# A two-block transformer on one core: attention, mixers and the entry to block 2 are issued in another order

## The chip, the cores and the metric

The kernel runs on one core of a Trainium2 chip. The metric is the device time of one execution in microseconds (us). Its engines each run their own list of instructions in the order written: TensorE (PE) multiplies, VectorE (DVE), ScalarE (ACT) and GpSimd (POOL, here also "Pool") work on vectors, SyncE (SP) issues the loads of weights. They wait for one another only through semaphores, so an instruction that waits holds up everything behind it on its engine.

## The reference

Two blocks follow one another on 256 tokens of width 1024, all in fp32. Block 1 has two layers, each with a feed-forward, a mixer (gated MLP in the first, attention in the second) and another feed-forward, with a second stream of 256 context tokens. Block 2 has two layers of feed-forward, mixer, feed-forward. Each sublayer is modulated by a vector m = silu(c) @ w_mod + b_mod.

```python
# block 1, layer 2: attention
qkv = h_lat @ w_qkv                      # 8 query heads, 2 key heads
q_l = apply_rope(rms_norm(split_heads(qkv[..., :Q_DIM], N_HEADS), q_norm_g), cos, sin)
y_lat = merge_heads(block_attend(q_l, k_all, v_all)) @ w_o

# block 2, each layer: the mixer between its two feed-forwards
h = _modulate(_rmsnorm(x, mix_norm[l]), sh2, sc2)
proj = h @ mix_w_in[l]
a_q, a_k, a_v, b_u, c_q, c_k, c_v, c_r, c_g = jnp.split(proj, splits, axis=-1)
o_a = _merge_heads(_moba_attention(rope(rmsnorm(a_q)), rope(rmsnorm(a_k)), a_v))   # 8 heads of 64
o_b = _conformer_conv(b_u, conv_w[l], ...)    # 31 taps, 256 channels, group norm, swish
o_c = _merge_heads(_rmsnorm(_gla(c_q, c_k, c_v, log_decay), gla_out_norm[l])) * jax.nn.silu(c_r)
x = x + gt2 * (jnp.concatenate([o_a, o_b, o_c], axis=-1) @ mix_w_out[l])
```

## The kernel before

**Products.** A fp32 operand a is split into a rounded high half and the rest, and each product is three passes: high by high, high by low, low by high. A "unit" is 1 MB of weights, loaded by SyncE in two transfers of 512 KB into one of two buffers `wraw`. ScalarE makes its high half `wh` (L838), VectorE its low half `wl` (L1228), and TensorE then runs the unit's products. SyncE may load unit u only when the low half of unit u-2 is made, since that is the last reader of the buffer. `split_next` issues a low half in VectorE's list; `unit(i)` there is a low half and, after it, the work on the unit's result.

**Modulation.** The vector m of the next sublayer is computed on VectorE while the present one runs: `modulation(i)` multiplies and adds (L1201, `acc`) one quarter `mraw` (1 MB) that SyncE loads in its queue between two units. TensorE's `columns` (L2099) sum the result over the partitions and turn it into columns.

**The order of the work** is written out by hand in one function for each engine and sublayer, with tables at the head of the file (`MIX_MODS`, `ATT_MODS`: after which unit a quarter comes; `MIX_TAPS`, `MIX_POOL_TAPS`: how many of the convolution's taps are done by when). No scheduler moves anything.

**Attention** (about 1680 to 1810 us). Units 0 to 3 give queries. For a pair of heads VectorE sums the squares (L1757), Pool raises the sum to the power -1/2, VectorE scales and rotates the queries in six operations (L1763 to L1773: "a turn"; `q_0` to `q_3`), TensorE transposes them (L2525) and ScalarE copies the result out of bank 6 of the result memory. Then for each head h: TensorE's scores, VectorE's maximum (`negm`, L1788), ScalarE's exponential, VectorE's division (L1793, L1796, "normalise"), TensorE's transposes of the weights (L2551) and ScalarE's copy `ptc_h`, TensorE's product with the values (L2566). The low halves of units 6 and 7 are made here by Pool (L796) and not by VectorE.

**Mixers of block 2** (about 2230 to 2410 and 2815 to 2991 us). After `proj` come the same steps for three kinds of heads: "a" and "b" (attention, `p_a`, `p_b`), "c" (the gated linear attention, `gla`), and "conv", whose 31 taps are shared by Pool (L809 multiplies, L815 adds, into `lnp`), VectorE and TensorE. Pool also makes the powers, placed between its taps after as many as `MIX_POOL_TAPS` says. Each part's result goes to the output product as a transposed, split left operand `xh`, `xl`; its low half is made on VectorE by L1935 (`low("gla")`, `low("conv")`, `low("att")`). `out(i)` is one of the four units of the output product (L2662), taken in the order `MIX_OUT`.

**Entry to block 2** (about 2009 to 2035 us). VectorE has the last result of block 1 copied out (`y_evac`), normalises it, and TensorE transposes it (L2140) and begins block 2's first feed-forward (L2365). `keep_going` is a run of throwaway products (L2128) that read constants and are read by nobody.

## Time and profile before

| | us |
|---|---|
| median of 3 runs (lowest, highest) | 3186.99 (3184.89, 3188.21) |
| profiled execution, its own time | 3188.7 |
| its span in the trace | 3187.0 |
| TensorE busy | 3090.6 (97% of the span) |
| mean granted clock of TensorE over the span, share of full | 0.984 |
| attention, mixer 1, mixer 2, entry: length of the stretch | 104, 120, 120, 28 |

The profiled execution took 1.7 us more than the median. In the trace, a "wait" is idle time of an engine ahead of an instruction, put down to the semaphore that came last by the profile; the engine named there may have been done for long, if the true one was a transfer. The granted clock is a share of full speed, at one of two levels (1.2 and 2.4 GHz) at any moment.

### The profile page before, as it was taken

How to read it: one execution, taken by the hardware profiler on the slowest of the kernel's cores; microseconds unless marked ns; L12 is line 12 of the kernel's file. 1: busy time of each engine (PE TensorE's matmuls, PEld its weight loads, DVE VectorE, ACT ScalarE, POOL GpSimd, SP SyncE). 2: the span in 40 equal slices, each digit the busy share in tenths (PEclk: the TensorE clock that was granted, in tenths of full speed). 3: DMA queues.
4: the chain of work that ended last, by engine and by line, in shares of the span. 5: the costliest groups of instructions: out<-in, count | busy, mean ns of one | idle time of the engine just before them, and what ended most of it. 6: DMA issues, size and time to landing. Idle time of an engine off the chain costs nothing.

```text
span 3187.0 us, 46876 instructions
## 1 busy us (share of the span) xinstructions
PE 3090.6 (97%) x19420; PEld 2751.5 (86%) x19420; DVE 2041.7 (64%) x2146; ACT 957.7 (30%) x1006; POOL 669.5 (21%) x616
## 2 busy tenths in 40 slices
PE   8999999999999999999997999999989999998999
PEld 5888889888888888888886798899879999997899
DVE  5844368666387434774556766675887758668664
ACT  2211122212222122221224433333533333354333
POOL 1311100224022010220102021330632313136110
PEclk9999999999999999999998999999999999999999
DMA  7633235332255332553523496685547868654464
GB/s 258 211 133 93 92 119 187 105 102 75 91 158 176 101 96 89 160 183 119 172 96 119 128 272 221 194 266 195 185 149 219 258 200 271 232 191 167 137 182 158
DMA packets 501669, 522.81 MB, mean 164 GB/s; under 512 B 15732, under 2 KB 433830, under 8 KB 501478
## 3 DMA queue, kind: packets, MB, share of 16 engines
q1 hardware_dynamic: 498536, 513.76, 50.4%
q0 software_dynamic: 2944, 6.32, 1.0%
q8 instruction: 144, 2.36, 0.3%
q14 instruction: 45, 0.37, 0.0%
HBM read 518.97 MB, written 1.05 MB: 163 GB/s over the span
## 4 chain that ended last, share of the span: by engine, by line
PE 86%; DVE 7%; POOL 3%; ACT 2%; DMA 1%; issue 1%; SPq 0%; DVEq 0%; ACTq 0%; POOLq 0%
PE ps L2191 29%; PE ps L2365 15%; PE ps L2277 15%; PE ps L2389 8%; PE ps L2219 6%; PE ps L2256 2%; DVE wl L1228 2%; PE ps L2235 1%; POOL wst L809 1%; PE ps L2662 1%; PE ps L2128 1%; POOL lnp L815 1%; PE ps L2303 1%; PE ps L2099 1%; DMA mraw<-in_ada_w 1%
## 5 line engine op out<-in xcount | busy, mean ns | idle before, releaser
L1228 DVE TENSOR_TENSOR wl<-wraw,wh 128x2048 fp32r<-128x2048 f32 x339 | 829.0, 2446 | 566.9 <-ACT wh L838 561.7
L838 ACT ACTIVATE wh<-wraw 128x2048 fp32r<-128x2048 f32 x341 | 652.5, 1913 | 945.7 <-PE ps L2277 387.5
L2191 PE MATMUL ps<-xh,wh 128*128 128x512 f32 (+1 forms) x1504 | 564.9, 376 | 0.5 <-DVE xl L1280 0.3
L2191 PE MATMUL ps<-xl,wh 128*128 128x512 f32 (+1 forms) x1504 | 552.7, 367 | 0.0
L2191 PE MATMUL ps<-xh,wl 128*128 128x512 f32 (+1 forms) x1504 | 551.3, 367 | 0.0
L2365 PE MATMUL ps<-xh,wh 128*128 128x258 f32 x1408 | 403.7, 287 | 5.3 <-DVE xl L1426 4.2
L2365 PE MATMUL ps<-xh,wl 128*128 128x258 f32 x1408 | 399.7, 284 | 0.0
L2365 PE MATMUL ps<-xl,wh 128*128 128x258 f32 x1408 | 399.3, 284 | 0.0
L673 POOL CAST hh<-ht 128x256 f32 (+1 forms) x176 | 140.1, 796 | 1227.1 <-DVE ht L1608 891.0
L1201 DVE SCALAR_TENSOR_TENSOR acc<-mraw,svec,acc 128x1024 f32<-128x1024 f32 x259 | 342.3, 1341 | 12.7 <-DMA mraw<-in_ada_w 5.2
L2191 PEld LDWEIGHTS ps<-xl,wh 128*128 128x128 f32 x1504 | 283.2, 188 | 49.3
L2191 PEld LDWEIGHTS ps<-xh,wl 128*128 128x128 f32 x1504 | 283.4, 188 | 44.9 <-issue 0.7
L2191 PEld LDWEIGHTS ps<-xh,wh 128*128 128x128 f32 x1504 | 283.6, 189 | 44.7 <-issue 1.4
L2365 PEld LDWEIGHTS ps<-xh,wh 128*128 128x128 f32 x1408 | 268.6, 191 | 10.3 <-DVE xl L1426 7.1
L2365 PEld LDWEIGHTS ps<-xl,wh 128*128 128x128 f32 x1408 | 269.0, 191 | 0.0
L2365 PEld LDWEIGHTS ps<-xh,wl 128*128 128x128 f32 x1408 | 268.7, 191 | 0.0
L2219 PE MATMUL ps<-wh,xh 128*128 128x256 f32 x832 | 241.4, 290 | 13.1 <-DVE wl L1228 13.1
L936 ACT ACTIVATE sg<-ps 128x512 f32<-128x512 f32 (+1 forms) x88 | 47.9, 545 | 662.3 <-PE ps L2191 629.8
L2219 PE MATMUL ps<-wl,xh 128*128 128x256 f32 x832 | 235.2, 283 | 0.0
L2219 PE MATMUL ps<-wh,xl 128*128 128x256 f32 x832 | 235.1, 283 | 0.0
L674 POOL TENSOR_TENSOR hl<-ht,hh 128x256 f32 (+1 forms) x176 | 214.5, 1219 | 29.1 <-POOL hh L673 29.1
L2277 PE MATMUL ps<-wh,hh 128*128 128x512 f32 x520 | 205.3, 395 | 1.3 <-DVE wl L1228 1.3
(430 smaller groups left out, 5564.6 us busy)
## 6 DMA issues: line engine op xcount, KB each, us to landing
wraw<-in_ffn_w_in SPq DMA_DIRECT2D x352, 512.0 KB, 5.2
wraw<-in_ffn_w_out SPq DMA_DIRECT2D x176, 512.0 KB, 4.2
mraw<-in_ada_w SPq DMA_DIRECT2D x72, 1024.0 KB, 7.0
mraw<-in_w_mod SPq DMA_DIRECT2D x64, 1024.0 KB, 6.8
wraw<-in_gmlp_w_in SPq DMA_DIRECT2D x48, 512.0 KB, 4.5
wraw<-in_mix_w_in SPq DMA_DIRECT2D x48, 512.0 KB, 4.7
wraw<-in_gmlp_w_out SPq DMA_DIRECT2D x24, 512.0 KB, 3.9
first_w<-in_w_mod SPq DMA_DIRECT2D x8, 1024.0 KB, 11.6
```

Of the source, the lines that this page charges most:

```text
L673: steps.link(pool.tensor_copy(hh[:, where], ht[:, par, 0:width]))
L674: pool.tensor_tensor(hl[:, where], ht[:, par, 0:width], hh[:, where].bitcast(F32), ALU.subtract)\
L838: act.activation(wh[:, slot], wraw[:, slot], ACT.Copy).then_inc(whi_done, 1)
L936: act.activation(sg[:, pair, 0:W], ps[:, 2 * pair, 0:W], ACT.Silu).then_inc(sg_ready, 1)
L1201: op = dve.scalar_tensor_tensor(out=to, in0=mraw[:, q % 2, jj], scalar=svec[:, v, 2 * q + jj:2 * q + jj + 1], in1=biasrow[:] if q == jj == ...
L1228: dve.tensor_tensor(wl[:, slot], wraw[:, slot], wh[:, slot].bitcast(F32), ALU.subtract)\
L2191: m = pe.matmul(ps[:, bank, 0:width], a, b, start=k == p == 0, stop=k == KD - 1 and p == 2)
L2219: m = pe.matmul(to, a, b, start=k == p == 0, stop=k == KD - 1 and p == 2)
L2256: m = pe.matmul(ps[:, 2 * t + half], a, b, start=False, stop=i == kk == 1 and p == 2, skip_group_check=i == 0)
L2277: m = pe.matmul(ps[:, bank0 + 2 * t + half], a, b, start=start and kk == p == 0, stop=stop and kk == 1 and p == 2, skip_group_check=not st ...
L2365: m = pe.matmul(ps[:, 2 * pair + r, 0:XW], a, b, start=n == p == 0, stop=n == KD - 1 and p == 2)
L2389: m = pe.matmul(ps[:, j, 0:T], a, b, start=i == kk == p == 0, stop=i == KF // 2 - 1 and kk == 1 and p == 2, skip_group_check=i == 5)
```

## The change

- **Attention.** The sums of squares are issued one unit ahead of the turns. The turn of `q_2` comes ahead of the first maximum, that of `q_3` after the third head's maximum in the loop over heads. Pool's two low halves go to VectorE, after heads 2 and 4. The second query unit is transposed through bank 7. ScalarE makes the high halves of units 5 and 6 earlier in its list, and an exponential of one column is put in ahead of unit 5.
- **Mixers.** Low halves move ahead of sums and statistics, and the quarters of modulation come after them. Pool's powers come after 7 and 10 taps instead of 9 and 13. ScalarE instead of VectorE copies the linear attention's output, squares it, and copies the turned weights; small activations of one column stand ahead of changes of its function. TensorE's output products wait for the copied convolution and no longer for its statistics. The columns of modulation move behind the scores and behind the last output product.
- **Entry to block 2.** 20 throwaway products run before the wait for `y_evac` and 36 after it, then the transposes, then the columns; before, the wait came first, then the columns, 16 throwaways, and the transposes.

The order in three places, before and after. First VectorE's list in attention, from the first head's maximum on (negm, from the scores in ps); nrm holds sums of squares, ql queries, den and sg or ht the softmax. Before:

```order
L1788 TENSOR_REDUCE negm<-ps 128x2
L1757 TENSOR_REDUCE nrm<-tm 128x4
L1483 TENSOR_SCALAR nrm<-nrm 128x4
L1763 TENSOR_TENSOR ql<-ql,nrm 128x2x256
L1768 TENSOR_TENSOR tm<-ql,wst 128x256
L1769 TENSOR_TENSOR tm<-ql,wst 128x256
L1770 TENSOR_TENSOR ql<-ql,wst 128x2x2x64
L1771 TENSOR_TENSOR ql<-ql,wst 128x2x2x64
L1772 TENSOR_TENSOR ql<-ql,tm 128x2x2x64
L1773 TENSOR_TENSOR ql<-ql,tm 128x2x2x64
L1793 RECIPROCAL den<-den 128x2
L1796 TENSOR_SCALAR sg<-sg,den 128x512 x2
```

After:

```order
L1786 TENSOR_TENSOR ql<-ql,tm 128x2x2x64
L1805 TENSOR_REDUCE negm<-ps 128x2
L1770 TENSOR_REDUCE nrm<-tm 128x4
L1496 TENSOR_SCALAR nrm<-nrm 128x4
L1810 RECIPROCAL den<-den 128x2
L1813 TENSOR_SCALAR sg<-sg,den 128x512 x2
L1805 TENSOR_REDUCE negm<-ps 128x2
L1810 RECIPROCAL den<-den 128x2
L1813 TENSOR_SCALAR ht<-ht,den 128x512 x2
L1805 TENSOR_REDUCE negm<-ps 128x2
L1776 TENSOR_TENSOR ql<-ql,nrm 128x2x256
```

The seven operations on ql no longer stand between the first maximum and the first division; the sum of `q_3` (nrm) alone does. The turn of `q_2` ends in the first row; that of `q_3` begins in the last.

Second, VectorE's list in each mixer, behind the turn of the queries (proj); modc and acc belong to modulation, nrm to the next heads' sum. Before:

```order
L1916 TENSOR_TENSOR proj<-proj,om 128x2x8x32
L1917 TENSOR_TENSOR proj<-proj,om 128x2x8x32
L1221 COPY modc<-ps 128x8
L1201 SCALAR_TENSOR_TENSOR acc<-mraw,svec,biasrow 128x1024
L1201 SCALAR_TENSOR_TENSOR acc<-mraw,svec,acc 128x1024
L1899 TENSOR_REDUCE nrm<-om 128x16
L1483 TENSOR_SCALAR nrm<-nrm 128x16
L1228 TENSOR_TENSOR wl<-wraw,wh 128x2048
L1201 SCALAR_TENSOR_TENSOR acc<-mraw,svec,acc 128x1024 x2
L1889 SCALAR_TENSOR_TENSOR wst<-lnp,wst 128x256 x3
L1907 TENSOR_TENSOR proj<-proj,nrm 128x2x512
```

After:

```order
L1937 TENSOR_TENSOR proj<-proj,om 128x2x8x32
L1938 TENSOR_TENSOR proj<-proj,om 128x2x8x32
L1239 TENSOR_TENSOR wl<-wraw,wh 128x2048
L1920 TENSOR_REDUCE nrm<-om 128x16
L1496 TENSOR_SCALAR nrm<-nrm 128x16
L1232 COPY modc<-ps 128x8
L1212 SCALAR_TENSOR_TENSOR acc<-mraw,svec,biasrow 128x1024
L1212 SCALAR_TENSOR_TENSOR acc<-mraw,svec,acc 128x1024
```

The low half wl of unit 7 has moved ahead of the sum and of two operations of modulation; the three taps (L1889) are no longer here.

Third, VectorE's list at the end of each mixer; lnp is the convolution, BN_STATS and BN_AGGR its statistics, xl the low half of the linear attention's result. Before:

```order
L1930 TENSOR_TENSOR sg<-sg,den 128x1024
L1921 TENSOR_REDUCE negm<-ps 128x4
L2048 COPY lnp<-ps 128x512
L2051 BN_STATS x<-lnp 128x6 x8
L2054 BN_AGGR x<-x 128x2 x8
L2056 TENSOR_SCALAR x<-x 128x8
L2059 TENSOR_TENSOR lnp<-lnp,x 128x512
L1935 TENSOR_TENSOR xl<-ps,xh 128x2x256
```

After:

```order
L1951 TENSOR_TENSOR sg<-sg,den 128x1024
L1239 TENSOR_TENSOR wl<-wraw,wh 128x2048
L2067 COPY lnp<-ps 128x512
L2070 TENSOR_TENSOR om<-om,gg 128x2x256
L1942 TENSOR_REDUCE negm<-ps 128x4
L1956 TENSOR_TENSOR xl<-ps,xh 128x2x256
L2074 BN_STATS x<-lnp 128x6 x8
L2077 BN_AGGR x<-x 128x2 x8
L2079 TENSOR_SCALAR x<-x 128x8
```

L1935 (now L1956) has moved ahead of sixteen BN operations and two that follow them. A low half of weights (L1239) has come in ahead of the convolution's copy.

```diff
@@ -55,7 +55,7 @@
 MIX_TAPS = (0, 0, 0, 6, 12, 18, 24, 31, 31, 31, 31, 31)
-MIX_POOL_TAPS, MIX_DVE_TAPS = (9, 13, 24), (24, 28, 31)
+MIX_POOL_TAPS, MIX_DVE_TAPS = (7, 10, 24), (24, 28, 31)
@@ -308,6 +308,7 @@
 nrm_g = place[:, 1944:1952]
+table_scrap = place[:, 1768:1772]
 tm_ang = place[:, 1880:1944].rearrange("p (t f) -> p t f", t=TT)
@@ -790,11 +791,6 @@
             power(nrm1[:, 4 * u:4 * u + 4], 4)
-        for i in (6, 7):
-            u = s["n_unit"] + i
-            pool.wait_ge(whi_done, u + 1)
-            pool.tensor_tensor(wl[:, u % 2], wraw[:, u % 2], wh[:, u % 2].bitcast(F32), ALU.subtract)\
-                .then_inc(wlo_done, 1)
     elif s["kind"] == "mix":
@@ -1001,7 +997,8 @@
             AP_.wait(act, "q_%d" % u, 0)
-            AA.done("qt_%d" % u, act.activation(qt1[:, 2 * u:2 * u + 2].rearrange("p a b -> p (a b)"), ps[:, 6], ACT.Copy))
+            AA.done("qt_%d" % u, act.activation(qt1[:, 2 * u:2 * u + 2].rearrange("p a b -> p (a b)"),
+                                                ps[:, 7 if u == 1 else 6], ACT.Copy))
@@ -1024,15 +1021,17 @@
         unit(3, False)
+        square(1)
         split_next(u0 + 4)
-        square(1)
-        copy_heads(0)
         unit(4, False)
         square(2)
+        copy_heads(0)
+        split_next(u0 + 5)
+        act.activation(nrm1[:, 31:32], ones[:, 0:1], ACT.Exp)
+        unit(5, False)
+        square(3)
         copy_heads(1)
         exps(0)
-        unit(5)
-        square(3)
         copy_heads(2)
@@ -1075,8 +1074,8 @@
                     act.activation(proj[:, :, at:at + CW], src, ACT.Copy).then_inc(pair_free, 1)
-            if i == 2:
-                split_next(u0 + 3)
+            if i in (2, 5, 6):
+                split_next(u0 + i + 1)
             if i < 10:
@@ -1136,8 +1135,8 @@
         square(1)
-        unit(6)
-        unit(7)
+        unit(6, False)
+        unit(7, False)
         split_next(u0 + 8)
@@ -1148,13 +1147,25 @@
         unit(10)
+        MP.wait(act, "o", turn)
+        stage("o_copy", act.activation(om[:, :, 768:1024], ps[:, 6].rearrange("p (t c) -> p t c", t=TT), ACT.Copy))
+        stage("o_sq", act.activation(hx[:], om[:, :, 768:1024], ACT.Square))
         exps("c", 2, p_c, 0)
-        unit(11)
+        split_next(u0 + 11)
         exps("b", 4, p_b, 8)
+        act.activation(table_scrap[:, 0:1], ones[:, 0:1], ACT.Silu)
+        unit(11, False)
+        act.activation(table_scrap[:, 1:2], ones[:, 0:1], ACT.Exp)
         MP.wait(act, "omt", turn)
...
         exps("a", 0, p_a[:], 12)
+        act.activation(table_scrap[:, 2:3], ones[:, 0:1], ACT.Silu)
+        MP.wait(act, "pt_c", turn)
+        MA.done("pt_c", act.activation(pt0[:, :, :, 0:P], ps[:, 2:4].rearrange("p r (h q) -> p r h q", h=4), ACT.Copy))
         unit(12)
+        MP.wait(act, "pt_b", turn)
+        act.activation(pt0[:, :, 2:4, P:2 * P], ps[:, 2].rearrange("p (r h q) -> p r h q", r=2, h=2), ACT.Copy)
+        MA.done("pt_b", act.activation(pt1[:, :, 2:4], ps[:, 3].rearrange("p (r h q) -> p r h q", r=2, h=2), ACT.Copy))
         MV.wait(act, "o_conv", turn)
@@ -1449,6 +1460,8 @@
                 take_chunk(s, n + 2)
+            if n == 5 and s["kind"] == "mix":
+                mod_end(nxt, 2, 3)
             low_chunk(nxt, n)
@@ -1776,11 +1789,15 @@
-        def queries(u):
-            part = nrm1[:, 4 * u:4 * u + 4]
-            sums("%d" % u, tm1[:, 2 + u % 2].rearrange("p (n d) -> p n d", d=HD), part)
-            dve.wait_ge(rstd_ready, n_power[0])
-            turn(ql[:, :, u * CW:(u + 1) * CW], part, 0, "q_%d" % u)
+        asked = {}
+        def query_sums(u):
+            sums("%d" % u, tm1[:, 2 + u % 2].rearrange("p (n d) -> p n d", d=HD), nrm1[:, 4 * u:4 * u + 4])
+            asked[u] = n_power[0]
+        def query_turn(u):
+            dve.wait_ge(rstd_ready, asked[u])
+            turn(ql[:, :, u * CW:(u + 1) * CW], nrm1[:, 4 * u:4 * u + 4], 0, "q_%d" % u)
@@ -1814,19 +1831,28 @@
         turn(ql[:, :, 1024:1280], k_part[:, 0:4], 1, "k_turned")
+        query_sums(0)
         unit(3)
-        queries(0)
+        query_turn(0)
+        query_sums(1)
         unit(4)
-        queries(1)
+        query_sums(2)
+        query_turn(1)
+        query_turn(2)
         maximum(0)
-        queries(2)
+        query_sums(3)
         normalise(0)
         maximum(1)
-        queries(3)
         normalise(1)
...
                 maximum(h + 2)
+            if h == 0:
+                query_turn(3)
+            elif h == 2:
+                unit(5)
+            elif h == 4:
+                unit(6)
             if h in ATT_MODS:
@@ -1834,7 +1860,6 @@
                 normalise(h + 2)
-        dve.wait_ge(wlo_done, u0 + 9)
         unit(7)
@@ -1857,12 +1882,8 @@
                 mod_end(nxt, 0, 6, 480)
-            if i == 9:
-                mod_end(nxt, 1, 6, 488)
             if i == 12:
                 factors(nxt)
-            if i == 15:
-                mod_end(nxt, 2, 3)
             for sec, q in mix_mods(i):
@@ -1974,20 +1995,19 @@
         turn_heads(0)
+        split_next(u0 + 6)
+        sum_squares(1)
         modulation(5)
-        sum_squares(1)
-        unit(6)
-        taps(1)
         turn_heads(1)
         split_next(u0 + 7)
-        split_next(u0 + 8)
-        modulation(7)
         MA.wait(dve, "decays", turn)
...
         stage("qk", dve.tensor_tensor(kt[:], c_k, e2[:], ALU.mult))
-        modulation(8)
+        modulation(6)
+        split_next(u0 + 8)
+        modulation(7)
         for j in range(2):
@@ -2004,7 +2024,9 @@
         stage("kt_t", op)
-        unit(9)
+        modulation(8)
+        split_next(u0 + 9)
+        mod_end(nxt, 1, 6, 488)
         MP.wait(dve, "scores", turn)
@@ -2024,29 +2046,30 @@
         stage("states", op)
-        unit(10)
+        split_next(u0 + 10)
+        taps(1)
+        modulation(9)
         maximum("c", 2, 8, 0)
-        MP.wait(dve, "o", turn)
+        MA.wait(dve, "o_sq", turn)
         o_c = om[:, :, 768:1024]
-        stage("o_copy", dve.tensor_copy(o_c, ps[:, 6].rearrange("p (t c) -> p t c", t=TT)))
-        steps.link(dve.tensor_tensor(hx[:], o_c, o_c, ALU.mult))
         groups = nrm_g.rearrange("p (t h) -> p t h", t=TT)
...
         maximum("b", 4, 4, 8)
-        unit(11)
         dve.wait_ge(rstd_ready, n_power[0])
...
                                      ALU.mult))
+        normalise("c", p_c, 0)
+        split_next(u0 + 11)
+        MP.wait(dve, "conv", turn)
+        stage("conv_c", dve.tensor_copy(ctok.rearrange("p a b -> p (a b)"), ps[:, 7]))
+        grp = ctok.rearrange("p t (g c) -> p (t g) c", c=64)
         MA.wait(dve, "silu", turn)
         stage("oc", dve.tensor_tensor(o_c, o_c, gg[:], ALU.mult))
-        normalise("c", p_c, 0)
         maximum("a", 0, 4, 12)
-        MP.wait(dve, "conv", turn)
-        steps.link(dve.tensor_copy(ctok.rearrange("p a b -> p (a b)"), ps[:, 7]))
-        grp = ctok.rearrange("p t (g c) -> p (t g) c", c=64)
+        low("gla", 6, (6,))
         for g in range(8):
@@ -2057,10 +2080,8 @@
         stage("stats", dve.tensor_tensor(grp, grp, hmv[:, :, 0:1].broadcast_to([P, 8, 64]), ALU.subtract))
-        low("gla", 6, (6,))
-        MP.wait(dve, "pt_c", turn)
-        MV.done("pt_c", dve.tensor_copy(pt0[:, :, :, 0:P], ps[:, 2:4].rearrange("p r (h q) -> p r h q", h=4)))
         normalise("b", p_b, 8)
+        normalise("a", p_a[:], 12)
         dve.wait_ge(rstd_ready, n_power[0])
@@ -2068,16 +2089,15 @@
         stage("o_conv", last)
-        normalise("a", p_a[:], 12)
-        turned_weights("b", 2, slice(2, 4))
         turned_weights("a", 0, slice(0, 2))
...
         low("conv", 4, (2,))
+        split_next(u0 + 13)
+        low("att", 0, (0, 1))
+        modulation(10)
+        split_next(u0 + 14)
         modulation(12)
-        unit(13)
-        low("att", 0, (0, 1))
-        unit(14)
-        unit(15)
+        modulation(13)
     if s["block"] == 1 and not two(nxt):
@@ -2336,10 +2356,11 @@
     elif s["i"] == B2:
+        keep_going(3, 20)
         pe.wait_ge(y_evac, s["n_group"])
+        keep_going(3, 36)
+        transposes(s)
         columns(s, 2)
-        keep_going(3, 16)
-        transposes(s)
     now[:] = halves_of(s)
@@ -2516,13 +2537,13 @@
             AV.wait(pe, "q_%d" % u, 0)
-            if u in (1, 2):
-                AA.wait(pe, "qt_%d" % (u - 1), 0)
+            if u == 2:
+                AA.wait(pe, "qt_0", 0)
             elif u == 3:
...
                 for t in range(TT):
-                    m = pe.transpose(ps[:, 6, h * T + t * P:h * T + (t + 1) * P],
+                    m = pe.transpose(ps[:, 7 if u == 1 else 6, h * T + t * P:h * T + (t + 1) * P],
                                      ql[:, t, (2 * u + h) * HD:(2 * u + h + 1) * HD], ident[:])
@@ -2554,7 +2575,9 @@
             AA.wait(pe, "ptc_%d" % h, 0)
-            if h == 1:
+            if h == 0:
+                AA.wait(pe, "qt_1", 0)
+            elif h == 1:
                 AA.wait(pe, "qt_2", 0)
@@ -2665,8 +2688,6 @@
             m.then_inc(w_used, 1)
-            if i == 2:
-                columns(nxt, 2, 3)
@@ -2744,8 +2765,6 @@
         unit(9)
-        pe.wait_ge(mcol_done, sections(nxt, 0) + 1)
-        columns(nxt, 1, 6, 488)
         taps(9)
@@ -2761,6 +2780,8 @@
         MP.done("scores", m)
+        pe.wait_ge(mcol_done, sections(nxt, 0) + 1)
+        columns(nxt, 1, 6, 488)
         unit(10)
@@ -2792,14 +2813,14 @@
         MA.wait(pe, "exp_b", turn)
-        MV.wait(pe, "stats", turn)
+        MV.wait(pe, "conv_c", turn)
         out(0)
-        MV.wait(pe, "pt_c", turn)
+        MA.wait(pe, "pt_c", turn)
         MV.wait(pe, "norm_b", turn)
...
         MP.done("pt_a", turn_weights(p_a[:], 0))
-        MV.wait(pe, "pt_b", turn)
+        MA.wait(pe, "pt_b", turn)
         MA.wait(pe, "conv", turn)
@@ -2816,6 +2837,7 @@
             out(i)
+        columns(nxt, 2, 3)
 for n in range(8):
```

## Rows read from the trace of the kernel before

**Rows 1.** The page's part 1: busy time and share of each engine.
```profile
PE 3090.6 (97%) x19420; PEld 2751.5 (86%) x19420; DVE 2041.7 (64%) x2146; ACT 957.7 (30%) x1006; POOL 669.5 (21%) x616
```
**Rows 2.** TensorE's waits: line, releaser, us in total, times, longest.
```profile
PE ps L2662 <- DVE xl L1935: 19.8, 4, 6.1
...
PE ps L2219 <- DVE wl L1228: 13.1, 8, 4.3
...
PE ps L2551 <- DVE ht L1796: 7.3, 1, 7.3
PE ps L2525 <- DVE ql L1773: 6.0, 1, 6.0
```
**Rows 3.** Stretches: length, busy (x instructions) of five engines, TensorE clock, DMA share, GB/s.
```profile
1706.00:1810.00 104.00, 82.79 (x414) 63.04 (x413) 74.47 (x108) 40.50 (x66) 14.25 (x8) 0.90 0.32 108
2294.00:2414.00 120.00, 100.61 (x722) 92.53 (x721) 93.31 (x123) 42.62 (x77) 47.55 (x34) 0.90 0.42 139
2876.00:2996.00 120.00, 102.07 (x759) 94.32 (x757) 98.49 (x129) 44.95 (x79) 48.52 (x35) 0.93 0.42 141
2008.00:2036.00 28.00, 23.21 (x134) 21.60 (x133) 20.20 (x34) 8.53 (x15) 4.58 (x6) 0.76 0.27 84
```
**Rows 4.** VectorE on tile ql: ns min/median/max of the five turns' first two operations.
```profile
L1763 DVE TENSOR_TENSOR ql<-ql,nrm x5: 691/694/4992, 1701.7 to 1735.7; 128x512 f32<-128x512 f32 x5
L1768 DVE TENSOR_TENSOR tm<-ql,wst x5: 424/426/4597, 1702.4 to 1740.7; 128x256 f32<-128x256 f32 x5
```
**Rows 5.** GpSimd's timeline in attention: start us, us, line, operation.
```profile
1735.61 9.41 POOL L796 TENSOR_TENSOR wl<-wraw,wh 128x2048 fp32r<-128x2048 f32 x2
```
**Rows 6.** TensorE's timeline in attention; in brackets the idle time before.
```profile
1737.94 1.44 PE L2566 MATMUL ps<-ptb,ql 128*128 128x256 f32 x4 [2.92 <-ACT ptb L1043]
...
1748.39 1.97 PE L2551 MATMUL ps<-ident,ht 128*128 128x128 f32 x8 [7.30 <-DVE ht L1796]
```
**Rows 7.** ScalarE's timeline in attention.
```profile
1735.07 1.91 ACT L838 ACTIVATE wh<-wraw 128x2048 fp32r<-128x2048 f32 x1
```
**Rows 8.** DMA issues around attention: count, KB each, median us to landing.
```profile
mraw<-in_w_mod SPq DMA_DIRECT2D x4, 1024.0 KB, 6.3
```
**Rows 9.** TensorE's timeline in the second mixer.
```profile
2883.65 0.58 PE L2219 MATMUL ps<-wh,xh 128*128 128x256 f32 x1 [4.33 <-DVE wl L1228]
...
2931.91 0.60 PE L2785 MATMUL ps<-ident,lnp 128*128 128x128 f32 x4
...
2947.18 0.55 PE L2662 MATMUL ps<-xh,wh 128*128 128x256 f32 x1 [4.33 <-DVE xl L1935]
...
2971.70 0.55 PE L2662 MATMUL ps<-xh,wh 128*128 128x256 f32 x1 [5.00 <-DVE xl L1935]
```
**Rows 10.** VectorE's timeline in the second mixer.
```profile
2870.96 1.22 DVE L1907 TENSOR_TENSOR proj<-proj,nrm 128x1024 f32<-128x1024 f32 x1 [5.47 <-POOL nrm L670]
...
2946.34 0.69 DVE L1935 TENSOR_TENSOR xl<-ps,xh 128x512 fp32r<-128x512 f32 x1
```
**Rows 11.** GpSimd's timeline in the second mixer: the end of its taps.
```profile
2920.64 0.74 POOL L820 TENSOR_TENSOR lnp<-lnp,wst 128x256 f32<-128x256 f32 x1
```
**Rows 12.** GpSimd's taps of both mixers: ns min/median/max, first and last start.
```profile
L809 POOL TENSOR_SCALAR wst<-lnp x46: 921/1762/3895, 2262.8 to 2918.8; 128x256 f32<-128x256 f32 x46
L815 POOL TENSOR_TENSOR lnp<-lnp,wst x46: 722/1142/2670, 2263.8 to 2919.8; 128x256 f32<-128x256 f32 x46
```
**Rows 13.** TensorE's timeline at the entry to block 2.
```profile
2011.44 3.37 PE L2099 MATMUL ps<-ones,acc 128*128 128x1 f32 x16 [2.38 <-DVEq L1323]
2014.67 5.65 PE L2128 MATMUL ps<-ident,ones 128*128 128x128 f32 x32
...
2024.17 0.36 PE L2365 MATMUL ps<-xh,wh 128*128 128x258 f32 x1 [2.11 <-DVE xl L1426]
```
**Rows 14.** VectorE at that entry: the last normalising step.
```profile
2016.56 1.53 DVE L1360 TENSOR_SCALAR x<-x,mv,rstd 128x1024 f32<-128x1024 f32 x2 [0.84 <-POOL rstd L670]
```
**Rows 15.** TensorE at the entry to attention: 16 throwaway products at full clock.
```profile
1672.91 3.73 PE L2128 MATMUL ps<-ident,ones 128*128 128x128 f32 x32
```

14 lines of the change are left out of this document (7 added, 7 removed).

## The prediction

> **What bounds the kernel now.** I read the page's busy table first. TensorE is busy for 97% of the span, VectorE for 64%, the others for less [rows 1]. So a change in order can give back only two things: TensorE's idle time, and work that ran at a low clock behind it. Next I read TensorE's waits over the whole span. Four lines of them lie in the stretches that the diff touches: 19.8 us in four waits of the mixers' output products for a low half `xl`, 13.1 us in eight waits for low halves of weights, 7.3 us for head 1's weights, 6.0 us for `q_2` [rows 2]. Third, the table of stretches gives the whole of it: in attention TensorE is busy 82.79 of 104 us, in the mixers 100.61 and 102.07 of 120, at the entry 23.21 of 28, with a mean granted clock of 0.90, 0.90, 0.93 and 0.76 [rows 3]. Idle time is thus 21.2, 19.4, 17.9 and 4.8 us, 63 us in all. The level is either full or half, so a mean of 0.90 over 104 us is about 21 us at half clock; some of those are idle anyway, the others lose half of themselves. Last I read the timelines of the engines that end each wait [rows 4 to 14].
>
> **Attention, -9 us.** VectorE's turn of `q_3` contains two operations of 4.99 and 4.60 us whose medians are 0.69 and 0.42 [rows 4]. In the same time Pool's weight subtraction takes 9.41 us, started 0.06 us before them [rows 5]. The excess, 4.3 + 4.2 = 8.5 us, stands right ahead of head 1's division in VectorE's list, and TensorE waits 7.30 us for that [rows 6]. The change takes away both ends of this: the subtraction is VectorE's now, and the turn of `q_3` is behind three maxima. So 7.3 goes. The wait for `q_2`, 6.0 [rows 2], goes too: its turn now stands ahead of the first maximum, and its power is asked for a unit earlier.
> Low clock: of some 21 us at half level I count 13 as idle; the other 8 or 9 lose half, 4.5 us. Sum of what can be had: 17.8.
> Against it: head 0's maximum comes behind a turn of one operation of 0.69 and six of 0.42, 3.2 us [rows 4]; between 0 and that I take 1.3. Two low halves in VectorE's loop over heads, formerly Pool's: they cost what its idle time there doesn't cover, taken as 0.8. SyncE's queue: the load of unit 9 needs unit 7's low half, which now comes after head 4, and a quarter of modulation is loaded behind it. A quarter of 1 MB takes 6.3 us to land with nothing before it [rows 8]; VectorE will ask for the third one early, hold up the maximum behind it, and so TensorE. I take 4.3 us (0 to 6.3). Another dip of the clock from these waits: 2.4. ScalarE still makes a high half of 1.91 us ahead of head 0's copy [rows 7], so the wait of 2.92 [rows 6] stays. 17.8 - 1.3 - 0.8 - 4.3 - 2.4 = 9.0. Ends: all the costs absent, 16; every cost at its upper end and no clock back, 3.
>
> The Trainium skill says in *SBUF — State Buffer* (section "SBUF: two separate sides") that VectorE and GpSimd share a port pair as an exclusive lock, the loser being blocked for the whole instruction. By that rule the trace agrees: two short operations end with the long one of Pool.
>
> **The mixers, -18.4 and -15.9 us.** The second one shows the chain. VectorE's sum for the second turn asks Pool for a power, and Pool has taps ahead of it: VectorE stands idle 5.47 us until 2870.96 [rows 10]. It then turns, does two pieces of modulation, and makes unit 7's low half, for which TensorE waits 4.33 us at 2883.65 [rows 9]. The change asks Pool after 7 taps instead of 9. A tap is a multiplication and an addition, median 1.76 + 1.14 = 2.9 us [rows 12], so the power comes 5.8 us earlier, of which the sum's own place lets about 4.5 through; and the low half stands ahead of the sum and of a modulation's copy and products. Together it comes about 9 us sooner, and the wait of 4.33 goes. At the end of the mixer `out(0)` waits 4.33 and `out(2)` 5.00 us for `xl` [rows 9]. The first of these low halves runs at 2946.34 for 0.69 us [rows 10], behind the statistics, and needs nothing of them; the second stood behind modulation. Both have moved ahead. What is left of the idle time lies in smaller waits behind the same two chains.
> So I take the idle time as the whole that can be had, 19.4 and 17.9, and of the clock: a mean of 0.90 over 120 us is 12 us lost at most, 0.93 is 8.4, part of that on idle time; I take 7 and 6. Then I leave 8 us in each: 0.7 for the first `xl` itself [rows 10], about 1 for the copies that ScalarE now makes in a list with others, 0.5 at the feed-forward behind, up to 1.5 for Pool (below), 1 for a dip of the clock, and 3 because VectorE has little room: it is busy 98.49 us of the 120 [rows 3], and some 4 us of copies and squares leave it, so a stretch of 102 us would see it busy for 94 and any late input of it shows. 19.4 + 7 - 8 = 18.4; 17.9 + 6 - 8 = 15.9.
> The moved modulation quarters cost VectorE nothing more in sum; they lie beside TensorE's output products, and part of them behind the mixer, where it has room (64% busy over the span, [rows 1]). ScalarE gets one copy, one square, two copies of weights and small activations with their table loads, all from VectorE's side, with 30% busy [rows 1]. Pool's taps end at 2920.64 + 0.74 = 2921.4 [rows 11]; TensorE's transposes of them begin at 2931.91 [rows 9]. With 4.33 and about 4 of other idle time gone ahead of them, TensorE arrives at about 2923.6, so Pool is early by 2 us or, with denser neighbours, late by 1.5.
> Ends of the unknown: each mixer 10 (half of it turned into other waits) to 25 (nothing left over but the rest of the low clock).
>
> **The entry, +0.5 us.** Before: a wait of 2.38, columns of 3.37, 16 throwaways of 5.65 at 2014.67, the transposes, a wait of 2.11 for `xl`, and the first unit at 2024.17 [rows 13]. At full clock 16 of them take 3.73, 0.23 each [rows 15]. Now 20 (4.7 us) begin 2.38 before 2011.44, and cover that wait with 2.3 to spare; 36 more are 8.4, so the transposes begin at about 2022, against 2020.3, though VectorE's last normalising step ends at 2018.1 [rows 14]. That costs 1.7. The columns now lie in the wait of 2.11 and cost some 0.5 beyond it. Back come the part of the first unit at a full clock, 1.5 to 2, since TensorE has not stood still before it (the mean is 0.76 now, [rows 3]). Net +0.5, between -2.5 (more of the unit at full clock) and +2.
>
> In *TensorE: Matmul & The Clock Gate*, section "Part 4: PE-mode transpose", the Trainium skill says that transposes don't count as activity for the clock. Then the 16 transposes behind the throwaways would bring the clock down again ahead of the first unit, and the entry would cost 1.5 to 2 us; no row here separates that.
>
> **Sum.** -9.0 - 18.4 - 15.9 + 0.5 = -42.8, against the profiled execution's 3188.7: 3145.9. That execution lies 1.7 above the median of 3187.0, so 3144 beside the median.
>
> **Rivals.**
> A, half of it in the mixers. When the low halves come early, VectorE's and Pool's lists are denser and slow each other. Pool's longest tap operations are 3.90 and 2.67 us, its shortest 0.92 and 0.72 [rows 12], which shows how wide this is. For it: the 98.49 busy us of VectorE [rows 3] would be nearly the whole of a shorter stretch. Against it: each of the four large waits has one named instruction that no longer stands in front. Gain 9 + 10 + 10 = 29: 3158. Chance 0.29.
> B, the clock holds throughout and the quarter in attention is not late: -16, -23, -23 and +1: 3126. For it: TensorE would have no wait above 2 us left. Against it: some new wait has mostly taken an old one's place. Chance 0.14.
> C, slower: Pool's taps become the bound. TensorE needs all of Pool's taps before the transposes at 2931.91 [rows 9]. Pool's powers come earlier and push 14 to 17 taps behind them, beside a VectorE that now works there without a pause. If Pool ends at 2931.9, 10.5 after its present end, the gain ahead of the transposes is gone; 17 taps do that at 10.5 / 17 = 0.6 more each, 3.5 us instead of 2.9. The kernel becomes slower than before when the mixers lose 4.3 us each in place of gaining about 17, so at some 21 us behind TensorE's new arrival: 23 after Pool's present end, 1.4 more a tap, 4.3. At 4.6 a tap it is -9 + 0.5 + 2 x 8 = +7.5: 3194.5. The two longest together are 6.6 [rows 12], so it could be. Against it: the medians sum to 2.9, and the shared-side stalls were long only where a whole weight tile was subtracted [rows 4, 5], as none is on Pool now. Chance 0.06.
> D, it does not do what it says: each moved low half still waits for a load or high half behind it in another queue, and the waits reappear at the same size. Only attention's 7.3 would go: 3180. Chance 0.02.
>
> **Numbers.** The forecast has 0.49, A 0.29, B 0.14, C 0.06, D 0.02. What can be told from no change is about 0.2%, 6.4 us: faster is under 3180.6, slower over 3193.4. The forecast, A, B and half of D are faster; of C a third is within the 0.2%. Faster 0.93, same 0.03, slower 0.04. Range: the lower ends of the gains are 3 + 10 + 10 - 2 = 21 (3164), the upper 16 + 25 + 25 + 2 = 68 (3117); not all of them fall together, and I leave 1 in 10 on either side: 3123 to 3165.
>
> **What would show it.** In the profile after: VectorE's operations of a turn all near 0.69 and 0.42, none over 2; no wait of TensorE at the product that transposes `q_2`; the clock in attention over 0.95. In the mixers: unit 7's product behind less than 1 us of wait, the sum of waits for `xl` at the output product under 7 instead of 19.8, busy time of over 112 in what were 120 us, a clock of 0.97. The wait for Pool's taps ahead of the transposes at most 2 us. In attention a wait for a quarter `mraw` in VectorE's third modulation, which was not there. At the entry no idle time before the throwaways and a first unit without its half-speed part. I am wrong if VectorE waits for scores or powers at the same places a few us later, if Pool's tap chain ends last at the transposes, or if the stretches keep a mean clock of 0.90 though their waits have gone.

## The result and the profile after

The changed kernel takes 3137.16 us (median of 4 runs, 3135.3 to 3143.24), the kernel before 3185.94 on the same chips (4 runs). The ratio is 0.985, with a 95% interval of 0.9833 to 0.9867: 49 us less, between 42 and 53. The profiled execution took 3135.57, against 3188.7 before.

The page after, busy time and share of each engine, the row of [rows 1]:

```profile
PE 3076.2 (98%) x19500; PEld 2740.4 (87%) x19500; DVE 2031.9 (65%) x2138; ACT 965.0 (31%) x1023; POOL 668.9 (21%) x614
```

TensorE's waits after (line, releaser: us in total, times, longest), which answer to [rows 2]; L2685 is the output product, L2239 the product of attention and mixers, L2572 the transposes of attention's weights, L2589 the product with the values:

```profile
PE ps L2572 <- DVE ht L1813: 4.9, 1, 4.9
PE ps L2589 <- ACT ptb L1042: 4.9, 4, 2.5
PE ps L2239 <- DVE wl L1239: 3.7, 5, 1.0
...
PE ps L2685 <- DVE xl L1956: 1.5, 2, 0.8
```

The 19.8 us ahead of the output products are 1.5, the 13.1 ahead of L2239 are 3.7, and the wait for the third query pair is in no row. One wait of 4.9 us is new in kind, though it stands at the same line as the 7.3 of before.

To see where the time came from, each stage is cut at the same product in both kernels; attention runs from the transposes at L2580 (L2603 after) to the seventh product at L2277 (L2297 after). Length, busy time of the five engines, granted clock, DMA share, GB/s; attention, mixer 1, mixer 2 in the kernel before:

```profile
1706.27:1779.80 73.53, 54.24 (x281) 40.39 (x279) 56.22 (x85) 34.48 (x62) 13.40 (x6) 0.86 0.30 108
2242.92:2416.64 173.72, 153.25 (x1115) 142.07 (x1113) 137.11 (x180) 77.25 (x129) 80.25 (x55) 0.93 0.51 175
2869.16:2998.12 128.96, 111.03 (x826) 103.05 (x825) 104.20 (x135) 49.60 (x82) 55.88 (x39) 0.93 0.42 142
```

The same in the changed kernel, and the entry over 28 us as in [rows 3]:

```profile
1703.30:1769.57 66.27, 53.67 (x280) 40.42 (x279) 52.39 (x85) 34.69 (x63) 3.59 (x4) 0.93 0.33 121
2230.88:2380.15 149.27, 143.37 (x1115) 134.20 (x1114) 134.20 (x175) 80.78 (x137) 81.38 (x55) 0.99 0.61 203
2832.69:2944.93 112.24, 107.22 (x827) 100.58 (x826) 97.93 (x128) 53.06 (x95) 56.91 (x40) 0.95 0.51 167
2002.00:2030.00 28.00, 27.52 (x209) 26.61 (x208) 18.90 (x34) 9.16 (x16) 7.56 (x10) 0.88 0.28 84
```

Read a row as length less TensorE's busy time (idle), and busy time against busy time with as many matmuls (what the clock gives back). Attention is 7.3 us shorter, 6.7 of it idle time and 0.6 clock. Mixer 1 is 24.4 shorter: its idle time falls from 20.5 to 5.9, and the same 1115 records take 153.25 and then 143.37 us. Mixer 2 is 16.7 shorter, 12.9 of idle time and 3.8 of clock.

The stages sum to 47.5 us less (the entry is 0.9 longer), while the two profiled spans differ by 53.1. The other 6 us lie where TensorE's products are the same in both: 2.9 ahead of attention, where only the kernel before was at half clock around 45 and 448 us, and 3.2 between the entry and mixer 1, where it was at half clock around 2230 us. They belong to these two executions and not to the change.

The same cuts through every run, with the us of the stage at the half clock in brackets; "entry" is a stretch of 79 us from the feed-forward ahead of the entry (1954.4 in the kernel before) into block 2's first feed-forward (2033.4):

| run | median us | attention | entry | mixer 1 | mixer 2 |
|---|---|---|---|---|---|
| before | 3186 | 73.5 (20.5) | 79.0 (13.7) | 173.7 (23.9) | 129.0 (17.1) |
| after | 3137.2 | 66.3 (9.7) | 79.9 (6.8) | 149.3 (3.4) | 112.2 (10.2) |
| e1_att_only | 3174.5 | 66.4 (9.6) | 77.5 (10.2) | 173.6 (23.9) | 129.0 (17.1) |
| e2_mix_only | 3143.3 | 76.4 (17.1) | 79.4 (13.7) | 150.0 (6.8) | 110.9 (6.8) |
| e3_entry_only | 3184.5 | 74.0 (20.5) | 78.6 (0) | 168.2 (17.1) | 129.1 (17.1) |
| e4_powers_only | 3178.6 | 76.2 (17.1) | 77.5 (10.2) | 164.5 (13.7) | 122.6 (10.2) |
| e5_quarter | 3132.0 | 58.9 (0) | 80.2 (6.8) | 150.0 (6.8) | 108.7 (3.4) |
| e6_entry22 | 3134.4 | 66.5 (9.9) | 75.5 (3.4) | 151.8 (10.2) | 109.6 (6.8) |
| e7_powers_back | 3152.4 | 66.1 (5.8) | 80.4 (6.8) | 158.0 (10.2) | 117.2 (6.8) |
| e8_halves_only | 3182.3 | 72.5 (16.3) | 78.1 (10.2) | 172.7 (23.9) | 128.9 (17.1) |
| e9_gla_behind | 3151.4 | 67.0 (10.2) | 78.7 (0) | 162.2 (20.5) | 116.8 (13.7) |
| e10_att_behind | 3140.4 | 66.4 (9.7) | 79.7 (3.4) | 156.0 (13.7) | 109.9 (6.8) |
| e11_entry0 | 3140.7 | 66.8 (10.2) | 78.5 (17.1) | 149.2 (3.4) | 112.4 (10.2) |
| e12_best | 3129.0 | 58.9 (0) | 76.8 (6.8) | 151.9 (10.2) | 110.3 (6.8) |

Three cautions come with it. Each row is one profiled execution, and that of e4 was the shortest of its 11 (3169.0 against a median of 3178.6). The clock moves by itself: mixer 1 has the same instructions in before and in e3_entry_only, yet it is 5.5 us shorter there, with 6.8 us less at half clock. And equal brackets don't make equal stages: attention has the same instructions in before, e3, e2 and e4, and takes 73.5, 74.0, 76.4 and 76.2 us. The longer two have less time at half clock, but head 1's wait is 8.5 us in them and not 7.3. So a difference of a few us between two such rows proves nothing alone; the medians and intervals settle it, taken as ratios, since the kernel before was measured beside each group of runs and its own median lay between 3182.5 and 3186.5.

### The profile page after: what moved, and what is told of

It reads as the page before. It is cut to its first block, busy times and chain, and to the rows that moved or that the text cites. A ratio compares the mean times of both kernels' runs of the same rounds, so it can differ in the third digit from the quotient of the medians.

```text
span 3133.9 us, 47043 instructions
## 1 busy us (share of the span) xinstructions
PE 3076.2 (98%) x19500; PEld 2740.4 (87%) x19500; DVE 2031.9 (65%) x2138; ACT 965.0 (31%) x1023; POOL 668.9 (21%) x614
## 4 chain that ended last, share of the span: by engine, by line
PE 91%; DVE 5%; ACT 2%; issue 1%; DMA 1%; SPq 0%; POOL 0%; DVEq 0%; ACTq 0%
PE ps L2211 30%; PE ps L2386 16%; PE ps L2297 15%; PE ps L2239 8%; PE ps L2410 8%; PE ps L2276 2%; PE ps L2255 1%; DVE wl L1239 1%; PE ps L2148 1%; PE ps L2323 1%; PE ps L2653 1%; PE ps L2119 1%; PE ps L2685 1%; PE ps L2513 1%; ACT wh L834 1%
## 5 line engine op out<-in xcount | busy, mean ns | idle before, releaser
L1239 DVE TENSOR_TENSOR wl<-wraw,wh 128x2048 fp32r<-128x2048 f32 x341 | 833.7, 2445 | 567.9 <-ACT wh L834 562.7
L2239 PE MATMUL ps<-wh,xh 128*128 128x256 f32 x832 | 239.4, 288 | 3.7 <-DVE wl L1239 3.7
L2239 PE MATMUL ps<-wl,xh 128*128 128x256 f32 x832 | 233.4, 281 | 0.0
L2239 PE MATMUL ps<-wh,xl 128*128 128x256 f32 x832 | 233.4, 281 | 0.0
L2297 PE MATMUL ps<-wh,hh 128*128 128x512 f32 x520 | 205.2, 395 | 1.3 <-DVE wl L1239 1.3
```

Source lines behind the costliest of these rows:

```text
L1239: dve.tensor_tensor(wl[:, slot], wraw[:, slot], wh[:, slot].bitcast(F32), ALU.subtract)\
L2239: m = pe.matmul(to, a, b, start=k == p == 0, stop=k == KD - 1 and p == 2)
L2297: m = pe.matmul(ps[:, bank0 + 2 * t + half], a, b, start=start and kk == p == 0, stop=stop and kk == 1 and p == 2, skip_group_check=not st ...
```

## The experiments

**The three parts, one at a time.** Each is the kernel before with the hunks of one part of the diff.

e1_att_only:

> The kernel before with the attention part of the change alone. Theory (the parts act apart from one another, and the two traces' landmarks give each its share): attention 7.1 us shorter by the landmarks, so a time 7 below the kernel before, the wait of 7.3 us for head 1's weights and that of 6.0 for the third query pair gone, a wait of some 5 us for a late quarter of modulation in their place. Rival 1 (the forecast's own size): 9 below. Rival 2 (the freed time is taken back by the clock): within 2 us of before.

3174.48 us (4 runs), ratio 0.9962 (0.9946 to 0.9977): 12 us less, between 7.3 and 17. By the cut attention is 7.2 shorter, and TensorE's two waits are replaced by one of 4.8 for the late quarter, as the theory had it. The forecast's 9 lies in the interval and the theory's 7.1 just under its lower end; rival 2 is out, the clock takes nothing back.

e2_mix_only:

> The kernel before with the mixers' part alone. Theory: the landmarks give 27 us in the first mixer (3 of them a dip of the clock at its start that the change has nothing to do with) and 17 in the second, so 41 to 44 below the kernel before. Rival 1 (the forecast's sizes): 34 below. Rival 2 (a share of it belongs to the entry's or attention's part, by the clock or the queue of loads): under 30 below.

3143.32 us (4 runs), ratio 0.9863 (0.9848 to 0.9878): 44 us less, between 39 and 48. The mixers' part alone is nearly the whole, and the two cuts, 23.7 and 18.1 us shorter, are those of the changed kernel within the clock's own movement. The theory's 41 to 44 holds; the forecast's 34 is too small.

e3_entry_only:

```diff
+keep_going(3, 20)
 pe.wait_ge(y_evac, s["n_group"])
+keep_going(3, 36)
+transposes(s)
 columns(s, 2)
-keep_going(3, 16)
-transposes(s)
```

> The kernel before with the entry's part alone. Theory: 36 throwaway products behind the wait end 3.3 us after the normalised x is there, so the first unit starts later, and it still runs at half clock: 1.1 to 1.3 us slower than before. Rival 1: the forecast's 0.5 slower. Rival 2: with the units behind it at full clock it gives time back, 1 to 2 us faster.

3184.54 us (11 runs), ratio 0.9994 (0.9985 to 1.0003): no difference that can be told. The interval reaches from 5 us faster to 1 slower: the forecast's +0.5 and rival 2 (1 to 2 faster, as the median is) lie in it, the theory's 1.1 to 1.3 slower just outside. Its profiled execution shows the entry at a clock of 1.00 over 28 us, where the changed kernel, with the same instructions, has 0.88; so the theory's "still at half clock" did not hold in it either. The three parts sum to 12 + 44 + 2 = 58 us against 49 together; with intervals of some 5 us either way on each, that is no proof of a loss between them.

**Attention: which operation blocked which.**

```diff
-for i in (6, 7):                         # GpSimd
-    pool.wait_ge(whi_done, u + 1)
-    pool.tensor_tensor(wl[...], wraw[...], wh[...], ALU.subtract)
+if h == 2: unit(5)                       # VectorE, in the loop over heads
+elif h == 4: unit(6)
```

e8_halves_only:

> The kernel before with one thing changed: the two low halves of weights that Pool made in attention are made by VectorE, after heads 2 and 4; all sums and turns stay where they were. Theory (Pool's long operation blocks VectorE's short ones): the two operations of 4.99 and 4.60 us fall to 0.69 and 0.42, TensorE's wait of 7.30 goes, the wait of 6.0 for the third query pair stays, the late quarter comes in: attention 3 us shorter or less. Rival 1 (they were long for another reason, such as their place in the list): they stay long. Rival 2: the late quarter eats all of it and the clock more, no change or slower.

3182.29 us (12 runs), ratio 0.9997 (0.9988 to 1.0005): no change that can be told, 4 us less at most. The mechanism is as the theory said. VectorE's first two operations of the five turns, ns min/median/max, which answer to [rows 4]:

```profile
L1758 DVE TENSOR_TENSOR ql<-ql,nrm x5: 691/691/694, 1701.8 to 1735.7; 128x512 f32<-128x512 f32 x5
L1763 DVE TENSOR_TENSOR tm<-ql,wst x5: 424/425/426, 1702.5 to 1736.4; 128x256 f32<-128x256 f32 x5
```

The turn of `q_3` stands where it stood, and with Pool's subtractions gone both long operations are gone. [Rows 5] holds two subtractions (x2), and the trace has them apart: 4.51 us from 1735.61 and 4.93 from 1740.08. VectorE's operation of 4.99 began 0.06 us after the first, that of 4.60, at 1740.70, 0.6 after the second; each ended 0.3 to 0.5 us after its own. That TensorE gains nothing is seen in the waits of its timeline in the same stretch:

```profile
1728.53 1.11 PE L2523 MATMUL ps<-ident,ql 128*128 128x128 f32 x4 [6.00 <-DVE ql L1768]
...
1774.46 1.97 PE L2549 MATMUL ps<-ident,ht 128*128 128x128 f32 x8 [4.99 <-DVE ht L1791]
```

The wait of 7.30 is gone, the one of 6.00 stays, and 4.99 us come in near the end. The late quarter eats nearly all of it, as rival 2 has it; the cut is 1.0 us shorter. The Trainium skill's rule, *SBUF — State Buffer*, section "SBUF: two separate sides", of an exclusive lock between VectorE and GpSimd, agrees with these rows: 4.99 and 4.60 us with a subtraction at work each [rows 4], 0.69 and 0.42 without.

**The late quarter.** In the changed kernel VectorE waits in the loop, and behind it TensorE:

```profile
1761.26 2.60 DVE L1212 SCALAR_TENSOR_TENSOR acc<-mraw,svec,acc 128x1024 f32<-128x1024 f32 x2 [5.66 <-DMA mraw<-in_w_mod]
```

```profile
1765.25 1.97 PE L2572 MATMUL ps<-ident,ht 128*128 128x128 f32 x8 [4.93 <-DVE ht L1813]
```

SyncE's queue shows why: one run of loads that ends at 1754.24 with the last weight unit, which had to wait for unit 7's low half (made from 1750.86), and only then both quarters:

```profile
1743.54 10.64 SPq L515 DMA_DIRECT2D wraw<-in_attn_w_o  x4
1754.24 0.94 SPq L500 DMA_DIRECT2D mraw<-in_w_mod  x2
```

e5_quarter changes one number:

```diff
-ATT_MODS, ATT_LOADS = (1, 3, 5, 6), (5, 5, 9, 9)
+ATT_MODS, ATT_LOADS = (1, 3, 5, 6), (5, 5, 8, 9)
```

> The changed kernel with one load moved: the third quarter of modulation is loaded ahead of the attention's last weight unit instead of behind it. Theory (the wait of 5.66 us of VectorE for that quarter, and TensorE's 4.93 behind it, come from the place in SyncE's queue, behind a load that waits for unit 7's low half): VectorE's wait and TensorE's wait of 4.93 gone, attention 5 us shorter, up to 8 with the dip of the clock behind it, so 3130 to 3133. Rival (VectorE would wait at the same place for another input, or the weight unit comes late instead): TensorE waits 2 us or more at the last units, and the time stays within 2 us of the changed kernel.

3131.99 us (4 runs), ratio 0.9844 (0.983 to 0.9858). The queue now has the quarter at 1741.70, between the two weight units, VectorE's wait for it is gone, and what remains is 1.11 us for the fourth, which TensorE doesn't feel:

```profile
1740.85 0.81 SPq L515 DMA_DIRECT2D wraw<-in_attn_w_o  x2
1741.70 0.43 SPq L500 DMA_DIRECT2D mraw<-in_w_mod  x1
1750.47 0.81 SPq L515 DMA_DIRECT2D wraw<-in_attn_w_o  x2
1751.33 0.43 SPq L500 DMA_DIRECT2D mraw<-in_w_mod  x1
```

```profile
1700.84:1759.73 58.89, 49.84 (x279) 37.72 (x279) 52.57 (x86) 34.72 (x63) 4.04 (x4) 1.00 0.37 135
```

Attention is 58.9 us long instead of 66.3, 7.4 less. The wait of 4.93 is gone, and waits for low halves of the query units are 1.3 longer, so 3.6 are idle time; 3.8 are the clock, now at full all through it (9.7 us at half before). The time can't show it: the medians differ by 5 us, the ratios by 2 only, and the intervals overlap. That TensorE's wait hung on the place in the queue is shown by the trace; what it is worth in time is not.

**The mixers: the power.** e4_powers_only is the kernel before with one line changed; e7_powers_back is the changed kernel with that line as before:

```diff
-MIX_POOL_TAPS, MIX_DVE_TAPS = (9, 13, 24), (24, 28, 31)
+MIX_POOL_TAPS, MIX_DVE_TAPS = (7, 10, 24), (24, 28, 31)
```

> The kernel before with one line changed: Pool's powers come after 7 and 10 taps instead of 9 and 13. Theory: VectorE's wait of 5.47 us before the second turn shrinks, and with it each mixer's wait for unit 7's low half of 4.3 us: 4 to 9 us faster in all. Rival 1 (the low half waits for what else stands ahead of it in VectorE's list): under 2 us. Rival 2 (Pool's later taps become the bound at the transposes of its sum): slower.

> The changed kernel with Pool's powers after 9 and 13 taps again. Theory (the earlier power is one needed link of the mixers' chain): VectorE's wait ahead of the second turn comes back with 3 to 5 us, TensorE waits at unit 7 to 9 or at the heads' transposes, 2 to 4 us in each mixer, 4 to 8 slower in all. Rival 1 (with the low halves ahead of the sums, VectorE's wait for the power lies beside work of TensorE and costs nothing): within 2 us. Rival 2 (Pool's later taps held up the end): faster.

e4: 3178.64 us (11 runs), ratio 0.9979 (0.9969 to 0.9988): 7 us faster, between 4 and 10. VectorE turns two groups of heads in each mixer, and it is the first turn (the prediction and the expectations call it the second) that waited for Pool. In mixer 1 its idle time there falls from 5.48 us to 0.56, and TensorE's eight waits for low halves of weights fall from 13.1 us, the longest 4.3, to 7.1, the longest 1.2; the output products' 19.8 stay at 19.6:

```profile
2281.14 1.23 DVE L1907 TENSOR_TENSOR proj<-proj,nrm 128x1024 f32<-128x1024 f32 x1 [0.56 <-POOL nrm L670]
```

```profile
PE ps L2219 <- DVE wl L1228: 7.1, 8, 1.2
```

e7: 3152.42 us (5 runs), ratio 0.9903 (0.989 to 0.9916), against 0.985 with the line: 15 us slower than the changed kernel by the medians and 17 by the ratios, roughly 10 to 24, more than the 4 to 8 of the theory, and some twice what the line gives in the kernel before. VectorE's timeline and TensorE's waits in e7:

```profile
2277.50 1.23 DVE L1928 TENSOR_TENSOR proj<-proj,nrm 128x1024 f32<-128x1024 f32 x1 [5.49 <-POOL nrm L671]
...
2293.80 1.23 DVE L1928 TENSOR_TENSOR proj<-proj,nrm 128x1024 f32<-128x1024 f32 x1 [2.83 <-POOL nrm L671]
```

```profile
PE ps L2754 <- DVE proj L1938: 9.3, 2, 4.7
...
PE ps L2239 <- DVE wl L1239: 5.9, 7, 2.3
```

The first row is the first turn, with the stall of before; the second turn now waits too, for the second power. With the low half moved ahead of the second turn, TensorE waits less for low halves and more for the turned heads themselves (L2754), 4.7 us in each mixer. The late power is the same stall in both kernels; the other moves took away what else TensorE would have waited for.

**The mixers: the two low halves at the end.**

```diff
-low("gla", 6, (6,))                      # e9: behind the statistics again
 for g in range(8): ... bn_stats, bn_aggr ...
 stage("stats", ...)
+low("gla", 6, (6,))
```

```diff
-low("att", 0, (0, 1))                    # e10: behind two operations
 modulation(10)
+low("att", 0, (0, 1))
```

> The changed kernel with the linear attention's low half behind the convolution's statistics again, all else as changed. Theory (TensorE's wait at out(0) is set by what stands ahead of this low half in VectorE's list): the four kinds of statistics operations, 1.10 + 0.65 + 0.17 + 0.74 and gaps, 2.9 us, come ahead of it, TensorE's wait at out(0) goes from 0.77 to 3.6 in each mixer, 6 to 8 us slower in all with the clock. Rival (out(0) would wait anyway, for its high half or for the weights): the wait stays under 2 us, no change.

> The changed kernel with the attention heads' low half behind the two modulation operations that now follow it. Theory: it is made 2.6 us later (two operations of 1.3), TensorE takes it up at once at out(2), so a wait of about 2.5 us comes back in each mixer, 5 to 7 us slower in all with the clock. Rival 1 (there is slack at out(2)): under 2 us. Rival 2 (VectorE would have to wait there for the quarter's load too, as it did 3.17 us in the kernel before): over 5 us in each mixer.

e9: 3151.39 us (4 runs), ratio 0.9894 (0.987 to 0.9918): 14 us slower than the changed kernel by both measures, roughly 5 to 23. The wait is what the four operations are worth, 2.9 us more in each mixer:

```profile
PE ps L2685 <- DVE xl L1956: 7.4, 2, 3.7
```

The time is more than twice the wait, though the theory's 6 to 8 is within the noise. The cuts say where it lies: mixer 1 is 12.9 us longer, with 20.5 us at half clock against 3.4, mixer 2 is 4.5 longer. How much of that low clock the waits brought, and how much this one execution had anyway, isn't shown.

e10: 3140.37 us (4 runs), ratio 0.9861 (0.9841 to 0.9881): no difference from the changed kernel can be told, though the interval would allow the theory's 5 to 7. The trace decides: the wait that the theory adds is not there, so rival 1 holds. The low half is made 2.4 us later, counted from `out(0)`, and TensorE takes it up with no wait:

```profile
2365.75 1.22 DVE L1956 TENSOR_TENSOR xl<-ps,xh 128x1024 fp32r<-128x1024 f32 x1
```

```profile
2366.87 0.28 PE L2685 MATMUL ps<-xl,wh 128*128 128x256 f32 x1
2367.11 0.36 PE L2685 MATMUL ps<-xh,wh 128*128 128x256 f32 x1
```

It ends at 2366.97, and the unit that needs it begins at 2367.11, behind the product of 2366.87, as it would have. So `out(2)` had about 2.5 us of slack, used up to the last. What made 5.00 us of wait before [rows 9] is shown by VectorE's rows ahead of that low half in the kernel before:

```profile
2960.96 2.60 DVE L1201 SCALAR_TENSOR_TENSOR acc<-mraw,svec,acc 128x1024 f32<-128x1024 f32 x2 [0.21 <-DVE prea L1267]
...
2967.82 2.60 DVE L1201 SCALAR_TENSOR_TENSOR acc<-mraw,svec,acc 128x1024 f32<-128x1024 f32 x2 [2.05 <-DMA mraw<-in_ada_w]
```

Two pieces of modulation stood in front of it, 5.2 us, and the second waited for its own load, 2.05 us here and 3.17 in mixer 1 (where TensorE's wait was 6.10). Without the load's 2.05 some 2.95 of the 5.00 would have been left, an estimate from these rows. One piece fits into the slack of 2.5, as e10 shows; two pieces and the load did not.

**The entry.** e6_entry22 is the changed kernel with `keep_going(3, 22)` behind the wait in place of 36; e11_entry0 has neither the 20 nor the 36.

> The changed kernel with 22 throwaway products behind the wait at the entry to block 2 instead of 36. Theory (they end 3.3 us after the last normalising step): transposes 3.2 us earlier, the first unit as much earlier, at half clock as now: the entry 3 us shorter. Rival 1 (the throwaways also carry the clock): more of the first units runs at half clock, and 1 to 3 us of that are lost again. Rival 2: VectorE's first operations behind the transposes set the pace, no change.

> The changed kernel with no throwaway products at the entry to block 2 at all. Theory (the first unit runs at half clock whether they are there or not, and TensorE's place is set by x): the transposes begin when x is ready, 3.3 us earlier than with 36, and the time is that of 22 throwaways, or up to 2 us longer for more half clock. Rival (they carry the clock through): 3 to 7 us slower than with 22, with a low clock from the wait on for 10 us or more.

In the changed kernel x is ready at 2008.2 (VectorE's last step begins at 2006.69 and takes 1.53), and the transposes begin at 2011.52, right behind the throwaways:

```profile
1999.01 12.67 PE L2148 MATMUL ps<-ident,ones 128*128 128x128 f32 x112
2011.52 1.91 PE L2160 MATMUL ps<-ident,x 128*128 128x128 f32 x16
```

e6: 3134.36 us (4 runs), ratio 0.9849 (0.9835 to 0.9863); the interval holds the changed kernel's 0.985. By the cut the entry is 4.4 us shorter than in the changed kernel, 3.2 of it the 14 throwaways at 0.23 each, the rest clock (3.4 us at half against 6.8), so the theory's 3 holds and rival 1's loss is not seen. That stands in the trace and not in the times. e11: 3140.67 us (4 runs), ratio 0.9858 (0.9838 to 0.9878), no difference from the changed kernel either. TensorE stands 9.20 us before the transposes, and these and the columns take 3.65 and 3.41 us, at half clock:

```profile
2012.36 3.65 PE L2160 MATMUL ps<-ident,x 128*128 128x128 f32 x16 [9.20 <-issue]
2015.80 3.41 PE L2119 MATMUL ps<-ones,acc 128*128 128x1 f32 x16
```

17.1 us are at half clock there, against 0 to 6.8 in the six kernels with 56 throwaways and 3.4 and 6.8 in the two with 42. That is the rival's picture and not the theory's: the throwaways do carry the clock. The entry is 78.5 us long, against 78.6 to 80.4 with 56 and 75.5 and 76.8 with 42: 36 behind the wait delay as much as they save, 22 come out ahead. This rests on one trace each; the times don't tell the three apart.

**Both together.** e12_best has the lines of e5 and e6.

> The changed kernel with both the earlier load of the third quarter and 22 throwaways instead of 36. Theory (the two act apart): 7 to 9 us less in attention and 3 to 4.5 less at the entry by the stages, so about 3126, under both kernels. Rival (the granted clock takes part of it back): 3130 to 3134.

3128.98 us (5 runs, 3128.27 to 3136.16), ratio 0.9831 (0.9813 to 0.9848): 54 us below the kernel before and, by the medians, 8 below the changed kernel, by the ratios 6. The intervals overlap (the changed kernel's is 0.9833 to 0.9867), so that last gain is not shown beyond the noise. Attention is 58.9 us again, 7.4 less than in the changed kernel, and the entry 76.8, 3.1 less, both as the theory had them. It has the lowest median of all runs here; the theory's 3126 was 3 too low, and the rival's 3130 to 3134 a little too high.

## Why the prediction was right

- **Direction, size and time.** 3144 was forecast, in a range of 3123 to 3165; 3137 came. 42.8 us against 49 (42 to 53). Part of the closeness is luck: attention and the entry gave 2 us less than written down and the mixers 7 more, and mixer 1's share moves by itself. Measured against its 168.2 us in e3, where it has the instructions of before, its gain is 19.0 and not 24.4.
- **Attention, -9.** 7.3 by the cut. The wait of 7.30 was Pool's doing (e8), the one of 6.0 went, head 0's new wait was put at 1.3 and is 1.49 us at TensorE, and the late quarter, put at 4.3, is 4.93. Idle time fell by 6.7 where these terms give 6.9. What was too large is the clock: 0.6 came back where 4.5 less a dip of 2.4 was written. The forecast took Pool's 9.41 us for one subtraction; it was two, one behind each long operation, which changes nothing in the sum. The quarter could have been had: e5 shows it was one place in a queue.
- **The mixers, -18.4 and -15.9.** 24.4 and 16.7, and together 44 in e2. The chain was right link by link: VectorE's wait for Pool's power ahead of the first turn is 0.55 us in mixer 2 instead of 5.47, of the waits of 4.33 that at unit 7 is gone and that at `out(0)` 0.77, and that of 5.00 at `out(2)` is gone. The term that was mis-sized is what is left over. 8 us were written down for each mixer, 3 of them because VectorE would be too dense. Idle time left is 5.9 and 5.0 in a longer cut, and VectorE, busy for 134.20 of 149.27 us and 97.93 of 112.24, holds TensorE up for 1.0 us at a time at most. ScalarE costs more than the "about 1" written for its copies: TensorE waits for it 1.3 and 0.9 us in each mixer, against 0.7 before. The other part of the miss is mixer 1's clock: 7 were given back in the sum, 9.9 came.
- **What it left out.** It put the wait at `out(2)` down to the place of the low half behind modulation, which is right but not the whole: 2.05 of the 5.00 us (3.17 in mixer 1) was the second piece's wait for its load. And e10 shows that in the changed kernel one piece could have stayed in front at no cost.
- **The entry, +0.5.** The cut says +0.9, with 3.3 us of late transposes and a first unit partly at full clock. The time cannot show it (e3).
- **Its own signs.** Most came: the turns at 0.69 and 0.42, waits for `xl` of 1.5, the wait for a quarter in the loop. Three did not: attention's clock is 0.93 and not over 0.95, mixer 2's 0.95 and not 0.97, and the first unit behind the entry still has a half-speed part (0.88 over 28 us).
- **Its sums.** The ends of the range come from gains of 21 and 68 us, which give 3166 and 3119 from 3187.0 and not 3164 and 3117. And attention with all costs absent is 17.8 by its own terms, not 16. Neither touches the forecast.
- **Rival A** (half in the mixers, since VectorE and Pool slow each other) fell with its mechanism: Pool's taps have medians of 1.77 and 1.13 us after, against 1.76 and 1.14 before [rows 12], and its work on them in mixer 2 takes 80.2 us from first to last instead of 78.7.
- **Rival C** (Pool's taps the bound) came nearer than the medians suggest, and not near enough. The last tap in mixer 2 and TensorE's transposes of the sum:

```profile
2885.53 0.72 POOL L816 TENSOR_TENSOR lnp<-lnp,wst 128x256 f32<-128x256 f32 x1
```

```profile
2888.75 0.60 PE L2806 MATMUL ps<-ident,lnp 128*128 128x128 f32 x4
```

Pool is 2.5 us early, where it was 10.5 early before [rows 9, 11]; the forecast had 2.

Open: what makes the clock fall in one execution and not in the next. The runs of one kernel differ by 8 us (the changed one, granted clock 0.990 to 0.994), by 11 in e8 and 12 in e9, and no experiment here was aimed at it. So what the waits cost in clock is known only as a sum with this noise. Whether transposes count for it, the forecast's question from *TensorE: Matmul & The Clock Gate* ("Part 4: PE-mode transpose") in the Trainium skill, stays open as well: the same 36 throwaways, 16 transposes and columns were followed by a first unit at half clock in the changed kernel (0.88 over 28 us) and by one at full clock in e3 (1.00).

## What to carry to other kernels

When an operation moves, follow its engine's queue of loads as well: two costs behind the large moves were a quarter that stood behind a blocked weight load (4.93 us of TensorE's wait), and a low half that stood behind an operation waiting for its load (2 to 3 us of it). Where TensorE is 97% busy, price a stall at its length and, for the clock behind it, anything from little to as much again or more (of the gain in attention and the two mixers, idle time is 6.7 of 7.3 us, 14.6 of 24.4 and 12.9 of 16.7), and remove all links of a chain together: the one line for Pool's powers was worth 7 us alone and 15 in company. Throwaway products to hold the clock pay only up to the moment when the real input is there.

## What the runs showed of the hardware

- Two subtractions of 128x2048 on GpSimd, 4.51 and 4.93 us, each held one VectorE operation, of 0.69 and 0.42 us, for 4.99 and 4.60. GpSimd's taps of 128x256, beside a VectorE busy for 87% of mixer 2 after the change, kept their medians within 0.02 us.
- Two waits of 2.9 us more went with 14 us more of time (e9, roughly 5 to 23), and in mixer 1 17 us more were at half clock.
- With the same instructions in mixer 1, the time at half clock was 23.9 us in three kernels and 17.1 in a fourth, and the stage 5.5 us shorter there. Attention, with the same instructions, took 73.5 to 76.4 us in four kernels.
- 16 transposes took 1.91 us at full and 3.65 us at half clock.
